# First feed-forward weight by Strassen's scheme, seven half products for eight, in a hybrid decoder layer on one core

## What is computed

```python
x = x + m @ w_o
h = rmsnorm(x, norm_mlp)
x = x + jnp.square(jax.nn.relu(h @ w_ff1)) @ w_ff2     # w_ff1 1024x4096, w_ff2 4096x1024
y = rmsnorm(x, norm_final)
```

## Time and profile before

| | |
|---|---|
| median of 3 runs | 1674.63 us (1673.78 to 1675.65) |
| profiled execution | 1675.57 us, span 1673.8 us |
| granted TensorE clock, mean | 0.998 |
| busy: TensorE, VectorE, ScalarE, GpSimd | 98%, 41%, 29%, 5% |
| output projection, products | 795.1 to 890.6 us |
| four up and three down quarters | 890.6 to 1556.0 us |
| last down quarter and final norm | 1556.0 to 1673.8 us |
| DMA, mean | 93 GB/s |

### The profile page before, as it was taken

The page is one execution under the profiler, slowest core; times in us unless marked ns, Lnnn a source line. Parts: engine busy times, 40 slices in busy tenths (PEclk is TensorE's granted clock), DMA queues, the critical chain, the costliest instruction groups (busy, mean ns, idle before and its releaser), DMA issues. The chain is left out here.

```text
span 1673.8 us, 28340 instructions
## 1 busy us (share of the span) xinstructions
PE 1640.2 (98%) x10667; PEld 1588.5 (95%) x10667; DVE 687.7 (41%) x1236; ACT 482.6 (29%) x925; POOL 79.1 (5%) x94
## 2 busy tenths in 40 slices
PE   7999999999989999999999999999999999999997
PEld 7899998899978999999999999999999999999997
DVE  6112123334644444333644353333333333333566
ACT  5212123443433443112323320133102320133223
POOL 0150000000000000000121000000000000000021
PEclk9999999999999999999999999999999999999999
DMA  5444564242267876342111111111111111111224
GB/s 164 129 122 131 167 191 124 84 132 80 76 171 185 197 184 174 128 127 70 48 50 38 50 38 50 45 43 41 47 50 38 50 38 50 38 51 38 63 69 152
DMA packets 237202, 155.87 MB, mean 93 GB/s; under 512 B 23982, under 2 KB 227590, under 8 KB 237146
## 3 DMA queue, kind: packets, MB, share of 16 engines
q1 hardware_dynamic: 208590, 124.00, 26.5%
q10 hardware_dynamic: 26268, 28.31, 5.0%
q0 software_dynamic: 2288, 2.80, 0.8%
HBM read 122.00 MB, written 35.43 MB: 94 GB/s over the span
## 5 line engine op out<-in xcount | busy, mean ns | idle before, releaser
L647 PE MATMUL bank<-xhi,wh 128*128 128x352 f32 (+1 forms) x1104 | 372.0, 337 | 4.1 <-DVE xlo L1577 2.0
L648 PE MATMUL bank<-xlo,wh 128*128 128x352 f32 (+1 forms) x1104 | 360.3, 326 | 0.0
L649 PE MATMUL bank<-xhi,wl 128*128 128x352 f32 (+1 forms) x1104 | 359.8, 326 | 0.0
L1123 ACT ACTIVATE wh<-wr 128x1024 fp32r<-128x1024 f32 (+1 forms) x142 | 144.6, 1018 | 432.4 <-PE bank L649 336.4
L1539 DVE TENSOR_TENSOR wl<-wr,wh 128x1024 fp32r<-128x1024 f32 (+1 forms) x142 | 181.6, 1279 | 189.0 <-ACT wh L1123 187.8
L648 PE MATMUL bank<-hlo,wh 128*128 128x368 f32 (+1 forms) x768 | 251.4, 327 | 0.0
L647 PE MATMUL bank<-hhi,wh 128*128 128x368 f32 (+1 forms) x768 | 250.6, 326 | 0.3 <-DVE rel L1963 0.3
L649 PE MATMUL bank<-hhi,wl 128*128 128x368 f32 (+1 forms) x768 | 250.1, 326 | 0.0
L647 PEld LDWEIGHTS bank<-xhi,wh 128*128 128x128 f32 x1104 | 207.4, 188 | 15.7 <-issue 7.6
L648 PEld LDWEIGHTS bank<-xlo,wh 128*128 128x128 f32 x1104 | 207.6, 188 | 0.0
L649 PEld LDWEIGHTS bank<-xhi,wl 128*128 128x128 f32 x1104 | 207.5, 188 | 0.0
(11 more groups left out here) (235 smaller groups left out, 2053.9 us busy)
## 6 DMA issues: line engine op xcount, KB each, us to landing
wr<-in_w_ff_dram SPq DMA_DIRECT2D x72, 512.0 KB, 3.9
wr<-in_w_in_dram SPq DMA_DIRECT2D x46, 512.0 KB, 4.2
d_T<-stg ACTq DMA_DIRECT2D x18, 544.0 KB, 2.8
kvc<-in_cache_kv_g_dram SPq DMA_DIRECT2D x16, 512.0 KB, 6.3
kvc<-in_cache_kv_g_dram SPq DMA_DIRECT2D x32, 256.0 KB, 7.2
d_tm<-tm ACTq DMA_DIRECT2D x12, 512.0 KB, 3.7
d_m<-bb ACTq DMA_DIRECT2D x8, 544.0 KB, 3.2
ml<-d_m SPq DMA_DIRECT2D x8, 544.0 KB, 4.1
```

The source lines that it names most:

```text
L647: pe.matmul(bank[c][:, 0:n], wh[st_.p][:, k, :], a, start=(k == 0), stop=False)
L648: pe.matmul(bank[c][:, 0:n], wh[st_.p][:, k, :], b, start=False, stop=False)
L649: last = pe.matmul(bank[c][:, 0:n], wl[st_.p][:, k, :], a, start=False, stop=(k == nk - 1))
L1123: act.activation(wh[st_.p][:, 0:nk, :], wr[st_.p][:, 0:nk, :], ACT.Copy).then_inc(w_hi, 1)
```

## The change

Only the first feed-forward weight's products get another scheme; the second weight's are regrouped to fit.

- The hidden features go in 8 groups (NG_F) of 512, each two pairs of 128-feature blocks. A pair of blocks with the 1024 input features and 1088 tokens is a 2x2 by 2x2 block product: weight parts A11 to A22 (4 even or odd input slices by one block), token parts B11 to B22 (4 slices by 544 tokens). Instead of eight half products a pair makes seven units (Winograd's form of Strassen's scheme). A unit is one weight part or sum times one token part or sum: 2 chunks of 272 columns, 4 slices, 3 matmuls, 24 in all. The first pair of group 0 keeps the eight half products, as four plain units of 48.
- VectorE makes four sums of weight parts per pair (`sum_1`, `sums_23`, `sum_4`) and five sums of products with PSUM (`add_products`, `add_12`); some sums are made by accumulating in PSUM. Two product sums are kept in `u2` and `u3`.
- Relu, Square and Copy are three ScalarE operations on 544 columns (`chain`), where one was VectorE's before.
- The four sums of token parts (`token_sums`) are made once, in `x2` itself, during the output projection, after ScalarE has scaled `x2` in place; their splits (`t_parts`, `t_lo_parts`) fill `tall`. GpSimd stores `x2` to DRAM (`d_x2`) first.
- The residual then passes through a ring of four tiles (`xring`): SP loads a tile, VectorE adds three chunks, SP stores it. Every group's down products have 4 slices for each of 8 blocks, so the residual is added to 7 times and once in the last passes, for 3 and once before.
- The last group's second weights are all split to own tiles (`lh`, `ll`), once for both passes.

```diff
-        def quarter_up(q, first):
-            with pe.Fori(first, 4) as i:
-                for p in range(2):
-                    for c in range(3):
-                        chunk(Step(S_MLP + p, (16, q), (2, i)), KD, c, hhi, hlo)
...
+        def unit_products(g, l, operand, k, c, out, start, stop):
+            a, b = operand[:, 0, k, HT * c:HT * c + HT], operand[:, 1, k, HT * c:HT * c + HT]
+            p = (l - 3) % 2
+            pe.matmul(out, uh[p][:, k, :], a, start=start, stop=False, skip_group_check=True)
+            pe.matmul(out, uh[p][:, k, :], b, start=False, stop=False, skip_group_check=True)
+            return pe.matmul(out, ul[p][:, k, :], a, start=False, stop=stop, skip_group_check=True)
+
+        def unit(g, l, operand, b0, fresh=True):
+            pe.wait_ge(u_lo, unit_at(g, l) + 1)
+            for c in range(2):
+                for k in range(KF):
+                    last = unit_products(g, l, operand, k, c, banks8[:, b0 + c, 0:HT], fresh and k == 0, k == KF - 1)
+            last.then_inc(u_done, 1)
...
+        def up_pair(g, q):
+            n, l0 = pair_at(g, q), 7 * q
...
+            unit(g, l0, hall[:, B11], bA)
...
+            unit(g, l0 + 1, tall[:, T2], bB)
...
+            unit(g, l0 + 2, tall[:, T3], bC)
...
+            unit(g, l0 + 3, tall[:, T1], bD)
+            pe.wait_ge(ev, n * 5 + 2)
+            unit(g, l0 + 4, tall[:, T4], bC, fresh=False)
+            pe.wait_ge(p1_a, n + 1)
+            unit(g, l0 + 5, hall[:, B21], bA, fresh=False)
+            pe.wait_ge(ev, n * 5 + 3)
+            unit(g, l0 + 6, hall[:, B22], bD, fresh=False)
+
+        def down(g):
...
+            for j, c in DOWN_ORDER:
...
+                if c == 0:
+                    pe.wait_ge(u_lo, unit_at(g, l) + 1)
+                if j == 0 and c < 2:
+                    pe.wait_ge(f_lo, g * 8 + (7 + c))
+                if j >= 2:
+                    pe.wait_ge(y_t, g * 24 + DOWN_POS[(j - 2, c)])
...
+        pe.wait_ge(h_lo, 7)
+        plain_unit(3, (B11, B12), 4, True)
 
         pe.wait_ge(sqa_p, 8)
...
+        with pe.Fori(1, NG_F - 1) as g:
+            up_pair(g, 0)
+            up_pair(g, 1)
+            down(g)
...
+        def chain(e, parity, tile, half, src=None):
...
+                act.activation(split2(r[:]), src, ACT.Relu).then_inc(f_a, 1)
+            else:
+                act.activation(r[:], r[:], ACT.Relu).then_inc(f_a, 1)
+            act.wait_ge(f_a, e * 2 + 1)
+            act.activation(r[:], r[:], ACT.Square).then_inc(f_a, 1)
+            act.wait_ge(f_a, e * 2 + 2)
+            act.activation(chain_out(fhi, tile, half), r[:], ACT.Copy).then_inc(f_hi, 1)
...
+            up_hi(g, q, 5)
+            act.wait_ge(ev, n * 5 + 3)
+            chain(n * 4 + 4, 0, 2 * q + 1, 1)
+            up_hi(g, q, 6)
+            act.wait_ge(ev, n * 5 + 4)
+            chain(n * 4 + 5, 1, 2 * q + 1, 0)
...
+                down_hi(g, 0)
+            act.wait_ge(u_done, up_at(g, l0 + 5) + 1)
+            chain(n * 4 + 6, 0, 2 * q, 0, two(bA))
...
+        def add_products(g, l, b0, src, out):
+            dve.wait_ge(u_done, up_at(g, l) + 1)
+            dve.tensor_tensor(split2(out[:]), two(b0), split2(src[:]), ALU.add).then_inc(ev, 1)
...
+            for j, c in DOWN_ORDER:
+                if isinstance(g, int) and g == 0 and j == 0:
+                    if c:
+                        inverse_squares(c)
+                    dve.wait_ge(r2_d, c + 4)
+                mlp_add(g, j, c)
+                if c == 2 and j < 6:
+                    down_lo(g, j + 2)
...
+        def token_sums(k):
+
+            b1, b2 = x2[:, 2 * k, :], x2[:, 2 * k + 1, :]
+            first, second = slice(0, HALF), slice(HALF, TOK)
+            dve.wait_ge(h_scaled, 2 * k + 2)
+            dve.tensor_tensor(b1[:, first], b1[:, second], b1[:, first], ALU.subtract).then_inc(t_d, 1)
...
+        def down_loads(g):
+            for j in range(KD):
+                if j < 4:
+                    down_load(g, j + 4, u_lo, unit_at(g, 14 + j) + 1)
+                else:
+                    up_load(DOWN_SLOT[j - 4], g + 1, 0, u_lo, unit_at(g, 14 + j) + 1)
+                sp.wait_ge(y_d, g * 24 + DOWN_POS[(j, 2)])
+                sp.dma_start(d_x2[j], xring[:, j % 4, :]).then_inc(xr_st[j % 2], 16)
+                if j:
+                    ring_load(g, j - 1)
...
+        for j in range(KD):
             pool.wait_ge(sq_a, j + 1)
+            pool.dma_start(d_x2[j], x2[:, j, :]).then_inc(x2_st[j % 2], 16)
             pool.tensor_tensor(ssqa[:], ssqa[:], sq2[:], ALU.add).then_inc(sqa_p, 1)
```

More of the change, by code:

```diff
@@ L610, in store @@
                 sp.dma_start(y_s.rearrange("b t d -> (b t) d"), yt[t % 3][0:SAMP, :]).then_inc(y_st[t % 3], 16)
[L612 to L625, removed]
+        for t in range(TILES):
             store(t)
@@ new lines, in down @@
+        def down(g):
+            first = isinstance(g, int) and g == 0
+            used = ((4, 5, 6), (7, 2, 3)) if first else ((0, 1, 2), (3, 4, 5))
+            for j, c in DOWN_ORDER:
+                l = 14 + j
+                p = (l - 3) % 2
+                if c == 0:
[4 more added lines that the diff above has]
+                    pe.wait_ge(y_t, g * 24 + DOWN_POS[(j - 2, c)])
+                t0, w = CH[c]
+                out = bank[used[j % 2][c]][:, 0:w]
+                for k in range(KF):
+                    a, b = fhi[:, k, t0:t0 + w], flo[:, k, t0:t0 + w]
+                    pe.matmul(out, uh[p][:, k, :], a, start=(k == 0), stop=False)
+                    pe.matmul(out, uh[p][:, k, :], b, start=False, stop=False)
+                    last = pe.matmul(out, ul[p][:, k, :], a, start=False, stop=(k == KF - 1))
+                last.then_inc(y_pe, 1)
@@ L1031, in _ @@
+        pe.wait_ge(h_lo, 7)
+        plain_unit(3, (B11, B12), 4, True)
         pe.wait_ge(sqa_p, 8)
-        pe.wait_ge(ones_p, 1)
+        pe.wait_ge(set_p, 6)
         pe.wait_ge(res_d, 24)
         for c, (t0, n) in enumerate(CH):
[L1035 to L1042, removed]
+            pe.wait_ge(taken[c], S_MLP)
+            pe.matmul(bank[c][:, 0:n], ones[:], ssqa[:, t0:t0 + n], start=True, stop=True).then_inc(n2_pe, 1)
@@ L1043, in products @@
+        pe.wait_ge(h_lo, 8)
+        plain_unit(4, (B21, B22), 4, False)
+        pe.wait_ge(r2_d, 3)
+        plain_unit(5, (B11, B12), 0, True)
+        plain_unit(6, (B21, B22), 0, False)
+        up_pair(0, 1)
+        down(0)
+        with pe.Fori(1, NG_F - 1) as g:
+            up_pair(g, 0)
+            up_pair(g, 1)
+            down(g)
+        up_pair(NG_F - 1, 0)
+        up_pair(NG_F - 1, 1)
+        def products(j, src, out, ks=range(KF)):
             t0, n = src
             for k in ks:
-                if split and k in (0, KD - 1):
-                    pe.wait_ge(f_lo, split[k > 0])
@@ L1047, in products @@
                 a, b = fhi[:, k, t0:t0 + n], flo[:, k, t0:t0 + n]
[L1048 to L1050 removed]
+                pe.matmul(out[:, 0:n], lh[:, j, k, :], a, start=(k == 0), stop=False)
+                pe.matmul(out[:, 0:n], lh[:, j, k, :], b, start=False, stop=False)
@@ L1051, in products @@
+                last = pe.matmul(out[:, 0:n], ll[:, j, k, :], a, start=False, stop=(k == KF - 1))
             return last
```

657 lines of the change are left out of this document (468 added, 189 removed).

## The result

The changed kernel takes 1650.55 us (median of four, 1648.85 to 1653.75) for 1674.89 before (median of four): a ratio of 0.9857, 95% interval 0.9845 to 0.9869, that is 24 us less. Forecast were 11 us less, 1664. The direction was right and the time lies inside the range, 1648 to 1686, but the gain is more than twice the one worked out. So the question is which terms of the sum were 13 us too dear.

What follows compares the result with a forecast made beforehand. TensorE, busy 98% of the span, was taken as the bound, so saved up products shorten the time. -36.4 + 6.4 + 13.6 + 3.5 + 1.9 = -11.0 us gave 1664 us, range 1648 to 1686.

Steps and rivals of the forecast that it cites:

- up products, 2712: Up stage: 2712 matmuls of 272 columns at 126.4 ns take 342.8 us, 36.4 less than 379.2.
- (a) entry: sum of squares, second unit: First group's start: sum of squares late by 1.0 us, second Strassen unit's weight split behind two token chains by 3.2.
- (a) entry: reciprocals: First down group: two reciprocals of 2.45 us on VectorE ahead of a weight remainder, +2.2 us.
- (b) eight joints: Start of each down group: serial chain of 11.1 us against 9.1 of cover, +1.7 us each, 13.6 in all.
- (c) tail: Last stretch: VectorE's final work, held by POOL additions, outlasts TensorE's shortened work; +2 to +5 us, taken as +3.5.
- (d) half clock at the entry: Behind the entry's 3.2 us stand the clock may halve: +1.9 us (0 to 1.9).
- pairs inside, ring, token sums: VectorE and ScalarE work inside pairs, the residual's DRAM ring and in-place token sums all stay hidden: 0 us.
- The floor: Rival, up stage: 272-column matmuls start no faster than some floor; at 146.5 ns near 1710 us; chance 0.10.
- the waits hide: Rival: joints and entry at their lower ends (6 and 1 us), no clock loss, 1649 us; chance 0.12.
- The engines' chain becomes the bound: Rival: 0.1 us more per hand-over loses units inside pairs too, 12 to 27 us, 1676 to 1691; chance 0.14.
- fetch stall: Rival: TensorE's longer loop bodies fetched again, 1 to 2 us at each of 5 turns, 1669 to 1674; chance 0.10.

Runs made afterwards that it cites:

- joint order: Changed kernel with each down group's first chunk multiplying the slice that finishes last at the end: 1648.67 us, ratio 0.9843 to the kernel before.
- entry order: Changed kernel with the second Strassen unit's weight split ahead of two token chains and two reciprocals moved where VectorE is idle: 1645.46 us, ratio 0.9829.
- second trace: The changed kernel run again without any edit, as base for the other runs: 1649.42 us, ratio 0.9854 to the kernel before.
- eight-unit run: Changed kernel with each Strassen pair's last unit multiplied twice, 24 more matmuls 15 times: 1690.25 us in one execution.
- 136-column run: Changed kernel with each 272-column matmul in the pairs' 105 units made as two of 136, 5040 for 2520: 2249.01 us in one execution.
- joint-and-entry run: Changed kernel with the last-finished slice multiplied last, the second Strassen unit's weight split earlier and two reciprocals moved: 1639.84 us, ratio 0.9790.

## Why the prediction was wrong

Its steps, in us against the kernel before. Measured values are of the first trace, whose execution is 1.7 us below the median; the 125.2 ns are a looped up stage without a wait, 42.08 / 336.

| step | forecast | measured | from |
|---|---|---|---|
| up products, 2712 | -36.4 (126.4 ns) | -39.7 (125.2 ns) | joint order |
| (a) entry: sum of squares, second unit | +4.2 | +3.9 | up stages less products, joints and the 1.65 us of the sum's matmuls |
| (a) entry: reciprocals | +2.2 | +1.4 | entry order, 48.82 to 47.41 |
| (b) eight joints | +13.6 | +5.8 | joint order |
| (c) tail | +3.5 | +2.1 (0.6 in the second trace) | 72.63 against 70.5; 1.5 of it is half clock |
| (d) half clock at the entry | +1.9 | 0 (1.5 in the second trace) | granted clock |
| pairs inside, ring, token sums | 0 | +0.4 | seven down stages, 333.6 less the 1.4, for 331.8 |
| not forecast: start of the output projection | 0 | -0.7 | 794.46 for 795.11, the same operations |
| sum | -11.0 | -26.8 | spans: -26.8 |

**The step that failed** is (b), as the prediction put it: "with eleven hand-overs, 1.7, it is 11.1 us". Half of the miss is there, 7.8 of 15.8 us. The hand-over of 0.16 us had been read from one pair of operations and used for eleven. The prediction did set shorter hand-overs apart for the tail, as those "of code without loops"; but it is not the loop that makes the price. In the same loops of the kernel before, Relu to product takes 0.03, and the difference is in the operation: where a register picks its tile, the address is worked out behind the wait. The groups of the changed kernel run in loops too, with fixed tiles. With 0.03 for 0.16 the chain is 1.4 us shorter, 9.7; it measures 9.7 (the fifth unit starts at 1113.36, the first down matmul at 1123.06), against 9.0 us of cover, three units of 24 x 125.2 ns. (The durations alone are 9.4 in both, and the 0.3 for overlap that the prediction took off besides is already in the measured gaps.) The 0.7 between them is what a looped up stage loses. Putting the address work back brings the joint to 1.1 us; fixing the tiles in the kernel before takes it out of the row itself.

**The products** were 1.2 ns too dear each, 3.3 us: the line through three widths, drawn 48 columns on. The floor below was estimated at 104 ns for a load and measured 112, so 272 columns stand 13 ns above it.

**The tail** had the right mechanism, with blocks of 4.8 us for the 5.2 forecast, and a first wait of 2.9 for 4. **The clock** term is what one such stretch costs, 1.5 us, but the stretch is not sure to come: the two traces of the changed kernel have one each, behind the tail's stand and behind the entry's, the eight-unit run has both (922.0 to 925.4 and 1655.9 to 1659.3 us), and how many are in the median is not known. **The entry** was near. **The pairs** and the ring cost nothing, as worked out: but for the entry's, no wait is listed inside a pair in any trace, save at the loop's turns of the 136-column run.

Of the rivals, "the waits hide" gave 1649 with a chance of 0.12, and the time that came is close to it, in part by luck: the joints did come at its 6 us (5.8), but not by hiding, and the entry cost 5.3 for its 1, while the products, which it left alone, gave 3.3 us. "The engines' chain becomes the bound" had been fed by the same wrong price; the joint-order run excludes it, where TensorE works through both pairs without a stand. No fetch stall shows in the changed kernel's loops: the six up stages are alike within 0.01 us. A longer body seems to meet this rival, though: in the run of 136 columns each turn has a stand of 3.2 us, where 1 to 2 were put down.

Open stays why the executions differ by several microseconds ahead of the output projection (stretches of half clock there explain part: 1.7 us in the joint-order trace, while 1.5 us lost at 496 us in the second trace are made good by 516), and what decides whether a given stand is followed by the lower clock.

## What to carry to other kernels

Price a hand-over between engines from several pairs of the trace, and ask of each whether the operation's address is computed from a loop register: a chain of fixed addresses passes on in 0.03 us, one of register-picked tiles in 0.13 to 0.16. Where a consumer needs several slices and one comes last, let it begin with the others: reordering one chunk's four products was worth 0.7 us at each of eight places. Before a matmul is made narrower, find the width below which its starts come no closer; here that lies between 136 and 272 columns. And look at what the added matmuls do to a loop's body: with twice as many in the up stage, each turn cost a stand of 3.2 us.

## What the runs showed that was not expected

- At 136 columns the floor came with a second price: behind a stand of 3.2 us at each of the loop's five turns the granted clock was 0.50 for 143 to 147 us, though TensorE was busy 145.8 of 146.8 us in such a stretch. The kernel took 2249 us where the floor alone gives some 1890 to 1900 (5040 starts of 112 ns for 2520 of 125); five up stages of 142.5 us for 75.0 make 337 of the difference, the stands 16.
- An operation whose tile a register picks starts 0.10 to 0.13 us later behind its wait, on ScalarE and on VectorE alike.
- A stretch of half clock behind a stand comes in one execution and not in another: behind the entry's 2.4 us wait in one, behind the tail's 2.9 in another, behind both in the eight-unit run; in the joint-and-entry run, whose tail still waits 2.9 us, there was none up to 1630 us, and with both stands gone none from 20 to 1625. The last 1 to 4 us of the span are at half clock in every trace.
